# Two layers on one core: the filter made inside a feed-forward stage, and three mixers woven together

## The reference, cut to what matters

```python
for i in range(DEPTH):                                   # 2 layers
    x = x + 0.5 * swiglu(rmsnorm(x, ...), gate, up, down)  # first feed-forward stage
    h = rmsnorm(x, mix_norm[i]) @ w_in[i]                # 14 tiles of 128 columns
    y_mla  = mla_mixer(...)      # attention, 8 heads: scores, softmax, values
    y_conv = conformer_conv_mixer(...)  # gate, 31 taps over 256 channels, layer norm, silu
    y_hy   = hyena_mixer(...)    # z = x1 * long_conv(v, k0); y = x2 * long_conv(z, k1)
    y = concatenate([rmsnorm(y_mla), rmsnorm(y_conv), rmsnorm(y_hy)])
    x = x + y @ w_out[i]
    x = x + 0.5 * swiglu(rmsnorm(x, ...), ...)           # second feed-forward stage
```

```python
hdn = sin(fr*(z @ w1 + b1)); hdn = sin(fr*(hdn @ w2 + b2)); hdn = sin(fr*(hdn @ w3 + b3))
h = (hdn @ w4).reshape(l, 2, 2, 256) * decay             # two orders, forward and backward
k = k / sum(abs(k))                                      # then its transform
```

## Time and profile before

| | us |
|---|---|
| median of 3 runs | 3727.18 (3717.93 to 3730.82) |
| the profiled execution | 3726.39 |
| its span | 3724.6 |
| TensorE busy | 3403.5 (91%) |
| GpSimd, VectorE, ScalarE busy | 1970.3, 1854.4, 760.9 |

### The profile page before, as it was taken

The page is one execution under the profiler, slowest core; times in us unless marked ns, Lnnn a source line. Parts: engine busy times, 40 slices in busy tenths (PEclk is TensorE's granted clock), DMA queues, the critical chain, the costliest instruction groups (busy, mean ns, idle before and its releaser), DMA issues.

```text
span 3724.6 us, 45696 instructions
## 1 busy us (share of the span) xinstructions
PE 3403.5 (91%) x14460; PEld 2633.1 (71%) x14460; DVE 1854.4 (50%) x2102; ACT 760.9 (20%) x1221; POOL 1970.3 (53%) x1148
## 2 busy tenths in 40 slices
PE   7999868789999999987788999978889999999997
PEld 6888645357888888764436888757767777778886
DVE  5331576654321432267555431375567767864323
ACT  3220101332210221110242221111112222212211
POOL 5666561126666666647004666534435455566664
PEclk9999979899999999997989999989999999999999
DMA  3333300013233233320001333311122222223322
GB/s 118 98 99 96 107 23 23 23 35 96 96 96 97 91 97 97 101 98 24 12 12 57 96 96 96 110 57 62 62 68 66 68 68 68 80 92 95 98 96 76
DMA packets 84570, 283.73 MB, mean 76 GB/s; under 512 B 9382, under 2 KB 17958, under 8 KB 83816
## 3 DMA queue, kind: packets, MB, share of 16 engines
q1 hardware_dynamic: 74016, 268.84, 22.9%
q10 hardware_dynamic: 10440, 13.41, 1.1%
HBM read 280.12 MB, written 2.10 MB: 76 GB/s over the span
## 4 chain that ended last, share of the span: by engine, by line
PE 74%; DVE 18%; issue 4%; ACT 2%; DMA 1%; DVEq 1%; ACTq 0%; SPq 0%
PE bank L520 21%; PE bank L525 21%; PE bank L524 21%; DVE y L1492 2%; PE bank L761 2%; PE bank L736 1%; DVE x_lo L1359 1%; PE bank L692 1%; DVE xbc L1750 1%; PE bank L644 1%; PE bank L676 1%; PE bank L750 1%; DVE scaled L1434 1%; DVE short L1479 1%; PE bank L862 1%
## 5 line engine op out<-in xcount | busy, mean ns | idle before, releaser
L428 POOL TENSOR_SCALAR w_hi<-raw 128x1024 fp32r<-128x1024 f32 x504 | 550.8, 1093 | 1639.8 <-PE bank L520 1633.0
L431 POOL TENSOR_TENSOR w_lo<-raw,w_hi 128x1024 fp32r<-128x1024 f32 x504 | 1270.3, 2520 | 42.0
L520 PE MATMUL bank<-x_hi,w_hi 128*128 128x512 f32 x2800 | 1117.4, 399 | 58.3 <-DVE x_lo L1359 36.6
L524 PE MATMUL bank<-x_lo,w_hi 128*128 128x512 f32 x2800 | 1099.4, 393 | 0.0
L525 PE MATMUL bank<-x_hi,w_lo 128*128 128x512 f32 x2800 | 1098.8, 392 | 0.0
L520 PEld LDWEIGHTS bank<-x_hi,w_hi 128*128 128x128 f32 x2800 | 532.8, 190 | 196.9 <-issue 68.6
L524 PEld LDWEIGHTS bank<-x_lo,w_hi 128*128 128x128 f32 x2800 | 532.3, 190 | 115.9 <-issue 7.0
L525 PEld LDWEIGHTS bank<-x_hi,w_lo 128*128 128x128 f32 x2800 | 531.4, 190 | 112.3
L520 PE MATMUL bank<-hidden_hi,w_hi 128*128 (+1 forms) x880 | 346.7, 394 | 0.0
L525 PE MATMUL bank<-hidden_hi,w_lo 128*128 (+1 forms) x880 | 345.0, 392 | 0.0
L524 PE MATMUL bank<-hidden_lo,w_hi 128*128 (+1 forms) x880 | 341.5, 388 | 0.0
(11 more groups left out here) (314 smaller groups left out, 3667.9 us busy)
## 6 DMA issues: line engine op xcount, KB each, us to landing
raw<-in_w SPq DMA_DIRECT2D x504, 512.0 KB, 3.5
dft<-in_dft ACTq DMA_DIRECT2D x2, 2048.0 KB
dft<-in_dft ACTq DMA_DIRECT2D x8, 512.0 KB, 4.2
x<-in_x SPq DMA_DIRECT2D x2, 1024.0 KB, 6.5
out<-x SPq DMA_DIRECT2D x4, 512.0 KB, 2.6
mask<-in_mask ACTq DMA_DIRECT2D x1, 1536.0 KB, 7.1
decay<-in_decay ACTq DMA_DIRECT2D x2, 512.0 KB
sel<-in_sel ACTq DMA_DIRECT2D x1, 768.0 KB, 4.2
```

The source lines that it names most:

```text
L428: nc.gpsimd.tensor_scalar(w_hi[:, s % 2, :], raw[:, s, :], 1.0, 0.0, ALU.mult, ALU.add).then_inc(w_rounded, 1)
L431: nc.gpsimd.tensor_tensor(w_lo[:, s % 2, :], raw[:, s, :], w_hi[:, s % 2, :].bitcast(F32), ALU.subtract).then_inc(w_split, 1)
L520: first = nc.tensor.matmul(out, hi_w, hi, start=start, stop=False)
L524: nc.tensor.matmul(out, hi_w, lo, start=False, stop=False)
```

## The change

The filter leaves the mixer. `filter_piece(f)` of each engine stands behind hidden tile f of the layer's first feed-forward stage: the three layers at tiles 0, 2 and 4, the taps and transform of the first order at tiles 6 to 9, those of the second at 10 to 13. That stage is written out tile by tile in place of a loop. The transform matrix lies where the hidden tiles from the 15th on come later. The tables and that matrix are loaded at the start of the stage (eight loads), and TensorE waits for them ahead of the first filter layer, VectorE ahead of the first hidden tile. The magnitudes are summed by products with a single column of ones, with the magnitudes as weights; 1/sum is applied after the inverse transform and no longer to the filter.

In the mixer TensorE goes from the input projection into one woven order: `head(h, first_unit, second_unit)` does one head of the attention and takes two pieces of the long convolutions between its parts. The scores have three banks in turn. ScalarE divides the probabilities by their sums. VectorE puts one of the 31 taps behind each maximum and each product of spectra. GpSimd's 31 taps are cut in two, with two blocks split between. The squares for the norms are summed on TensorE, and the output projection takes its blocks as they become ready: `out_pair(half, pair)`. Only the edges of the padded tiles are cleared.

```diff
+KEPT = 15
+SCORE_BANKS = (4, 5, 6)
+TURN_BANKS = (1, 2)
+MIX_BANK = 3
+HYENA_BANKS = (7, 0)
+TAP_BANKS = (5, 6)
+TAP_SUM_BANKS = (7, 4)
...
+                end = l * LAYER_BLOCKS + FFN_BLOCKS + IN_BLOCKS + 2
                 split_blocks(at, end)
-                long_conv(l)
-                at = end
+                long_conv(l, 0, TAPS // 2)
+                split_blocks(end, end + 2)
...
+            def filter_piece(f):
+                if f in (0, 2, 4):
+                    filter_layer(f // 2)
+                if f in (6, 10):
+                    o = (f - 6) // 4
+                    if o == 0:
+                        pe.wait_ge(filt_sine, c.next(filt_sine))
+                    filter_taps(o, 0)
+                    filter_taps(o, 1)
+                if f in (7, 11):
+                    o = (f - 7) // 4
+                    filter_taps(o, 2)
+                    filter_taps(o, 3)
+                    tap_sum(o, 0)
+                    tap_sum(o, 1)
+                if f in (8, 12):
+                    o = (f - 8) // 4
+                    filter_spectrum(o, 0)
+                    filter_spectrum(o, 1)
+                    tap_sum(o, 2)
+                    tap_sum(o, 3)
+                if f in (9, 13):
+                    o = (f - 9) // 4
+                    filter_spectrum(o, 2)
+                    filter_spectrum(o, 3)
+            def ffn_with_filters():
+                for f in range(FC):
+                    b = f % 2
+                    pe.wait_ge(pair_free, c.next(pair_free))
+                    project(bank[2 * b][:], arriving=5 if f == 0 else 0).then_inc(gate_ready, 1)
+                    project(bank[2 * b + 1][:]).then_inc(up_ready, 1)
+                    if f == 0:
+                        sum_squares()
+                    filter_piece(f)
...
+            def scores(h, t):
+                n = 4 * h + t
+                if n % 16 >= 3:
+                    after(probs_ready, n - 2)
+                nc.tensor.matmul(bank[SCORE_BANKS[n % 3]][:], mla_q[0:QK, h % 4, t * P:(t + 1) * P],
+                                 mla_k[0:QK, h % 4, :], start=True, stop=True).then_inc(scores_ready, 1)
...
+            def head(h, first_unit, second_unit):
+                if h == 3:
+                    mla_inputs(1)
+                    first_unit()
+                    mla_inputs_taken(1)
+                    turn(h, 0)
+                    turn(h, 1)
+                    scores(h + 1, 0)
+                    scores(h + 1, 1)
+                    scores(h + 1, 2)
+                else:
+                    if h < 7:
+                        scores(h + 1, 0)
+                        scores(h + 1, 1)
+                        scores(h + 1, 2)
+                    turn(h, 0)
+                    turn(h, 1)
+                    first_unit()
+                if h < 7:
+                    scores(h + 1, 3)
+                mix(h, 0)
+                turn(h, 2)
+                mix(h, 1)
+                turn(h, 3)
+                second_unit()
+                mix(h, 2)
+                mix(h, 3)
...
+                signal_transposes(0)
+                frequencies(0, 0)
+                frequencies(0, 1)
+                pe.wait_ge(tile_free, c.at(tile_free) + len(RING))
+                mla_inputs(0)
+                frequencies(0, 2)
+                mla_inputs_taken(0)
+                scores(0, 0)
+                scores(0, 1)
+                scores(0, 2)
+                frequencies(0, 3)
+                scores(0, 3)
+                inverse(0, 0, 0)
+                head(0, lambda: inverse(0, 0, 1), lambda: inverse(0, 1, 0))
+                head(1, lambda: inverse(0, 1, 1), nothing)
+                head(2, lambda: signal_transposes(1), lambda: frequencies(1, 0))
+                head(3, lambda: frequencies(1, 1), lambda: frequencies(1, 2))
+                head(4, lambda: frequencies(1, 3), lambda: inverse(1, 0, 0))
+                head(5, lambda: inverse(1, 0, 1), lambda: inverse(1, 1, 0))
+                head(6, lambda: inverse(1, 1, 1), conv_mean)
+                hyena_sum()
+                head(7, conv_variance, nothing)
+                after(norm_split, 3 + 2)
+                after(norm_rms, 4)
+                after(probs_ready, 32)
+                out_pair(0, 0)
+                after(norm_squared, 3 + 7)
+                ones_sum(TURN_BANKS[0], conv_squares).then_inc(norm_sum, 1)
+                after(norm_squared, 3 + 5)
+                ones_sum(TURN_BANKS[1], mla_squares, 0, 3)
+                after(norm_squared, 3 + 8)
+                ones_sum(TURN_BANKS[1], mla_squares, 3, 4).then_inc(norm_sum, 1)
+                after(mixed_copied, 8)
+                after(norm_rms, 6)
+                out_pair(1, 0)
+                after(norm_split, 3 + 4)
+                out_pair(0, 1)
+                out_pair(1, 1)
+                after(norm_split, 3 + 8)
+                for half in range(2):
+                    out_pair(half, 2)
+                    out_pair(half, 3)
...
+            def load_filters(l):
+                for to, src in ((layer_cols, io["layer_cols"][bass.ds(l, 1)].rearrange("a p n -> p (a n)")),
+                                (filt_z, io["filt_z"]),
+                                (filt_w, io["filt_w"][bass.ds(l, 1)].rearrange("a p n -> p (a n)")),
+                                (decay_back, io["decay_back"]), (decay_early, io["decay"][:, 0:TT // 2]),
+                                (decay_late, io["decay"][:, TT // 2:TT]),
+                                (filt_cos, io["dft"][0][:, 0]), (filt_sin, io["dft"][0][:, 1])):
+                    act.dma_start(to[:], src).then_inc(layer_loaded, 16)
...
-                act.wait_ge(layer_loaded, c.next(layer_loaded, 16 * 6))
...
+            def ffn_with_filters(stage):
+                reciprocal_rms()
+                dve.wait_ge(layer_loaded, c.next(layer_loaded, 16 * 8))
+                for f in range(FC):
+                    hidden_tile(f % 2, hidden_hi[:, f, :], hidden_lo[:, f, :])
+                    filter_piece(f)
+                c.add(taps_magnitude, 8)
+                absorb(stage + 1, 0.5)
...
+                def maximum(h, t, tap=True):
+                    dve.wait_ge(scores_ready, c.next(scores_ready))
+                    nc.vector.reduce_max(row_shift[:, t:t + 1], bank[SCORE_BANKS[(4 * h + t) % 3]][:], AX_X
+                                         ).then_inc(dve_step, c.add(dve_step))
+                    if tap and taken[0] < TAPS:
+                        long_tap()
+                    dve.wait_ge(dve_step, c.at(dve_step))
+                    nc.vector.tensor_scalar(row_shift[:, t:t + 1], row_shift[:, t:t + 1],
+                                            -QK ** -0.5, None, ALU.mult).then_inc(row_ready, c.add(row_ready))
...
+                def head(h, first_unit, second_unit=nothing):
+                    if h == 3:
+                        query_ropes()
+                        first_unit()
+                    for t in range(3):
+                        maximum(h + 1, t)
+                    if h != 3:
+                        first_unit()
+                    if h == 3:
+                        second_unit()
+                    maximum(h + 1, 3)
+                    if h != 3:
+                        second_unit()
+                    invert_sums(h + 1)
+                    mixed(h)
...
-    return out + down_blocks(np.concatenate([w_out[512:], w_out[:512]]))
+    out_half = down_blocks(np.concatenate([w_out[768:], w_out[512:768], w_out[:512]]))
+    return out + [out_half[n] for n in (0, 4, 1, 5, 2, 3, 6, 7)]
```

More of the change, by code:

```diff
@@ L1618, in mixer @@
[L1618 to L1624 removed]
+                short_tile(0)
```

996 lines of the change are left out of this document (560 added, 436 removed).

## The result

Four runs took 3676.1 us in the middle (3670.8 to 3686.0), beside 3724.6 for four of the kernel before: 0.9873 of it, with an interval from 0.9855 to 0.9892. A second set gave 0.9861 [0.9846, 0.9876]. The kernel is 1.3% faster, 48 us. The forecast was 3612 us, a gain of 115 us; the time lies in its range, and next to the rival "VectorE becomes the bound of heads 0 to 4" (3666).

What follows compares the result with a forecast made beforehand. TensorE bounds the feed-forward stages; time was to be won in two 455 us mixers. Per layer -27 - 77.4 - 15 + 48 + 3 = -68.4, twice -136.8, +22 gives -114.8: from 3726.4 to 3612 us, range 3545 to 3685.

Steps and rivals of the forecast that it cites:

- VectorE becomes the bound of heads 0 to 4: Rival for the woven part: VectorE's 31 taps delay ScalarE, some 27 us more per layer, 3666 us; chance 0.17.
- prediction's own signs of being wrong: Tap sums over 15 us, transform waits at tiles 8 and 12 over 3 us, or mixer clock under 0.8.
- The woven part and the output projection, 249.4 us: Mixer's attention, long convolutions and output: 205.4 us work, 36 waits, 8 clock; 264.5 before, a gain of 15 per layer.
- The list of waits, 36 us: TensorE's waits in the woven part, from signal copy to output-block norms, found by laying two written orders side by side.
- Elsewhere a head's chain lies beside 8 to 11 us: In other heads, the 5 to 6 us softmax chain lies beside 8 to 11 us of TensorE work.
- The clock in it, 8 us: In the woven part, a granted TensorE clock of 0.96, costing 8 us.
- over by head 4: Argument against VectorE as the bound in the woven part: its taps are over by head 4.
- The filter's pieces in the feed-forward, +48 and +3: First feed-forward stage: 48.0 us more TensorE work per layer, plus 3 for waits around the taps.
- pieces don't fit: Rival: filter pieces overrun the splits, 7 us waits at four places and slow tap sums, about 3645 us; chance 0.08.
- The input projection, -27: Mixer's input projection without filter layers: 22.7 us of waits, 2.8 for products, 1.5 for clock saved per layer.
- The filter section, -77.4: The filter section leaves the mixer, saving its whole 77.4 us per layer.
- The loads, +18 and +4: Filter loads land at about 52 us, costing 18 us once at program start; about 4 us in the second layer.

Runs made afterwards that it cites:

- the two moves of order: Changed kernel with head 4's last maximum ahead of head 3's second unit (alone 0.9858), and head 7's inverse and the first output remainders earlier on VectorE (alone 0.9835).
- `fill`: Changed kernel with 14 useless matmuls a mixer put into three of TensorE's waits; 0.9864 of the kernel before.
- `ropes`: Changed kernel with VectorE's query ropes of the first head group ahead of the second product of spectra, the tap between dropped; 0.9855 of the kernel before.
- `trig`: Changed kernel with the two 1 MB filter loads issued behind tile 3 and waited for only at tile 8; 0.9814 of the kernel before.
- run 1026: Not a run label: "run" is a verb here, and 1026 ns is the mean time of VectorE's taps beside GpSimd's in the changed kernel.

## Why the forecast was wrong, by its own steps

None of the prediction's own signs of being wrong came: the sums of magnitudes take 7 us, TensorE waits for no transform, and the mixer's clock is 0.92. They watched the moved filter; the step that failed had none.

- **The woven part and the output projection, 249.4 us: the step that failed.** Measured 271, 22 us more in each layer. The work was right (205.4; at a clock of 0.91, 223.0 busy). The list of waits, 36 us, was found by laying the written orders side by side for TensorE and VectorE; TensorE was idle for 48, and the clock took 18 where 8 were set down: 12 and 10 us more, the 22. What the list had: signal 1.7 (1.2), queries 4.0 (6.8), first head 7.1 (5.8), head 3 with the step into head 4 11.0 (13.2), hyena norm 4.5 (4.1), first output block 4.5 (6.1), later norms 3 (6.1). What it left out: ScalarE's turned copies in heads 1 and 2 (3.8). "Elsewhere a head's chain lies beside 8 to 11 us" had ScalarE's divisions in it, but not that a copy, in ScalarE's program, stands behind an exponential of the next head and so behind VectorE's queue. What makes the chains long is shown by leaving it out: without VectorE's taps the stretch is 255.3 us, what the forecast amounts to on these marks (249.4 and 5.7), and the two moves of order give another 11.2.
- **The clock in it, 8 us.** By the busy time it was 18 (223.0 for 205.4), but `fill`, which raised it, gave back no time clear of noise. The deeper error was to make the time a sum of TensorE's work, waits and clock, where chains over three engines set it: `ropes` took 4.4 us off the queries' wait, 5.3 us stood up at the first scores, and the stretch was 1.3 us shorter in one layer and 1.2 longer in the other.
- **The rival "VectorE the bound of heads 0 to 4"** (27 us a layer above the forecast, 3666 us) is nearest in number and mostly in cause: the taps alone are worth 18.8. But VectorE was not full; its taps lengthen chains that the order makes long. That the number came within 10 us is luck in part: it had neither the 12 us of the hidden tiles' address nor the 9 us at the next stages' starts, which are in the measured one. Its chance of 0.17 was too small, and its argument against ("over by head 4") was no argument, since the cost arises before.
- **The filter's pieces in the feed-forward, +48 and +3**: right. Of 59.8 in layer 2, 7.6 is the load, 2.4 the pace of `down`; 49.8 remain. The pieces themselves, from the first start of each to the projection behind it, are 45.8 in either layer; most of the rest is the half clock behind the load's wait, up to 1207.4 us. TensorE never waited for a piece at tiles 6 to 13, so the +3 fell away, and the rival "pieces don't fit" with it (its own terms, taken for both layers, add up to 3655 and not 3645). Sixteen records of the magnitudes' sums, and half a transform step:
```profile
135.11 1.95 PE L649 MATMUL bank<-ones,taps_abs 128*128 128x1 f32 x16
136.92 0.48 PE L539 MATMUL bank<-x_hi,w_hi 128*128 128x512 f32 x1
...
169.27 1.89 PE L662 MATMUL bank<-even_odd,filt_sin 128*128 128x256 f32 x8
171.00 1.89 PE L662 MATMUL bank<-even_odd,filt_cos 128*128 128x256 f32 x8
```
  (136.92 - 135.11)/16 = 0.113 us here; the 16 records at 154.8 us start 0.106 us apart. Two of each make 7.0 us for 64, between the 8.3 taken and the 6.8 that the Trainium skill ("TensorE: Matmul & The Clock Gate", section "LDWEIGHTS (loading the stationary operand)") led to as an estimate; a load of 128 columns with one column to stream costs what the page's columns/1.2 ns says, within 6%. A transform step is 2 x 1.73 = 3.46 us, not 3.69. (It is 8 matmuls in 16 records, and not 16 matmuls as the prediction and the text ahead of it call it, and the eight matmuls of one column there stand for four of 256 before, not two; the sum is not touched.)
- **The input projection, -27**: right. From 450 us on, the waits that stay are 2.9 us at its start and 1.9 for a sum; the stage ends 82 us after its first product.
- **The filter section, -77.4**: nothing contradicts it. A mixer's -93.4 is -26 and -77.4, with +6.5 for the woven part, and 4.6 us of wait at the next stage's start (1.07 before, 5.68 now), which leaves 1 us unexplained. That last wait comes with the new order of the output blocks; no run tried another.
- **The loads, +18 and +4**: the wait ended at 49.0 us, not 52, and was 15.6 long, 7.6 in layer 2. From the first issue to the end of the wait it was 12.7 us, as forecast (12.8), but the issues began at 36.4 and not at 39. As `trig` shows, 9.7 us of wait stay at the start without the large loads.
- **What no step had**: the hidden tiles' address. 528 down products by 0.0045 us are 2.4 us for each of five feed-forward stages, 12 us. Of the 59 that the profiled run lacks (55.7 gained for 114.8), the woven part is some 43, this 12 and the next stages' starts 9; the start of the program gave 6 back.

## What to carry to other kernels

When streams are woven together by hand, follow each wait backwards through all engines' programs, not only through the two that seem busy: what counts is what stands ahead of the releaser in its own queue. Then ask where the wait goes when it is taken away: of the queries' wait hardly anything was gained, of head 3's 8.7 us in 9.7, of the mixer's end 9.2 in 13.8. Know the scatter of the stretch that you read, too: here the same mixer takes 272.9 to 276.5 us. And when a tile is added to on-chip memory, look at what it moves: the pace of an untouched stage is one look at its count of records.

## What was not expected of the hardware

- **A matmul's pace depends on where its moving tile lies in SBUF.** Same instructions, full clock, no waits: 0.2267 us with the tile at 115840 (128 modulo 512), 0.2289 at 99264 (448), 0.2334 at 115712 (0). The merge of the last layer's mixer (`merged_hi`, `merged_lo`), untouched by the change but moved by 64 bytes by two small tiles, went from 0.2267 (140928, 128 modulo 512) to 0.2290 (140992, 192). `w_hi` and `w_lo`, from which the weights are loaded meanwhile, lie at 128 modulo 512 too. That the difference to them is what counts is a guess; only these four places were measured.
- **VectorE's taps and GpSimd's** run 1026 ns together and 827 ns with GpSimd's left out. The Trainium skill ("SBUF — State Buffer", section "SBUF: two separate sides") says that the two take a pair of ports in turn; the trace agrees, and the time of the kernel did not move measurably (0.9855 beside 0.9861).
- **TensorE's clock can be held up by useless matmuls** (0.91 to 0.94) **with no gain that the ratio shows** (0.9864 beside 0.9861). That the slow products behind waits lie in time that other engines need anyway fits this, but is not shown; these runs leave room for some 7 us.
